# Prompt attention in one stage over pairs of heads, scores formed twice, and the gates as projection chunks

## The chip, the core and the metric

The kernel runs on one core of a Trainium2 chip. Its engines run side by side, each its own instruction queue: PE (TensorE, matmuls and transposes), ACT (ScalarE), DVE (VectorE), POOL (GpSimd) and SP (SyncE, which here issues DMAs). Matmuls read SBUF and write PSUM, eight banks of 512 f32 columns; ACT and DVE read PSUM, POOL does not. The metric is the device time of one execution in microseconds.

## What is computed

One step of a two-layer encoder, for a prompt of 1,024 tokens and for 8 streams of 16 tokens with caches of 512. A layer projects the tokens, runs three kinds of attention with 8 heads of 64 each (A: forgetting attention, causal; B: a sliding window with sinks; C: latent attention, chunk-causal), gates each, mixes them and normalises:

```python
  h = x @ W_in  (one combined projection; columns split among all head groups and gates)
  A: forgetting attention (FoX), per-frame causal, logit[t,s] += F[t]-F[s], F = cumsum(log sigmoid(w_f.x+b_f))
  B: sliding-window GQA (window 128 = two whole chunks back + own chunk) with learned per-head sinks, rotary
  C: multi-head latent attention (RMS-normed KV latent, decoupled rotary key), block-causal chunk mask
  branch_n = W_n( mixer_n * silu(gate_n) ),  m = sum_n sigmoid(g_n) * branch_n,  y = m @ W_o
  x <- LayerNorm(alpha * x + y),  alpha = (2*DEPTH)^(1/4)
```

## The kernel before

`build` runs, for each layer, nine stages with a barrier of all engines behind each: `projections`, `forget_sums`, `latent_keys`, `prompt_attention` for A, B and C, `stream_attention`, `up_projection`, `output_projection`. Between stages data go through scratch tensors in HBM. P is 128; NT is 9 token tiles (8 of the prompt, PT, and one of the streams); KT is 8 tiles of the model width.

`projections` makes x @ W_in in 9 chunks of up to 512 columns. Products there are fp32r: weights and inputs are each split into a high and a low half (wh, wl, xh, xl), and a token tile is 8 x 3 matmuls of 512 columns (L351 to L353) with the tokens as the stationary operand. xh and xl are kept through the attention stages, because the 3,072 gate columns are left over for them.

`latent_keys` transposes the latents of each token tile and multiplies them, in f32, with the weights of C's queries, keys and values.

`prompt_attention` works on one head after the other, two in a loop turn. `prep` (L995) transposes its queries and keys to have their 64 to 96 features on partitions. `order`, a list made in Python and the same for PE, ACT and DVE, sets the sequence. For each tile `a` of 128 queries: `score` (L1009, mask L1012) makes up to 1,024 columns of scores in PSUM (ss) with queries on partitions, DVE takes the row maximum (L1133), ACT the exponential and its sum (L1091), `turn` (L1027) transposes the probabilities tile by tile, ACT and DVE copy them out, and `pv` (L1045) multiplies them with the values, 64 columns at a time. DVE divides and gates (L1172). Between these, `fill` (L1056 to L1058) makes one token tile of 256 gate columns, 24 fp32r matmuls, nine times in a loop turn; POOL splits the gate weights (L968, L970).

`up_projection` transposes the three gated outputs of each token tile on PE (L1800), splits them and multiplies with W_n (L1820 to L1822).

## Time and profile before

| | us |
|---|---|
| median of the runs shown | 3794.53 |
| lowest and highest of three | 3792.19, 3799.66 |
| the profiled execution | 3789.74 |
| its span, first instruction to last | 3788.1 |

A profile row gives an engine's busy time, a count, and in the groups the mean length of one. A PE record's length holds its way through the array, some 0.16 us, so a matmul's price is the distance from one start to the next. An f32 matmul leaves two records, an fp32r or bf16 one leaves one. `128*64` behind the names is the stationary operand, rows by columns; PEld is its load. PEclk is the granted share of the clock: 1.0 stands for 2.4 GHz, 0.5 for 1.2.

### The profile page before, as it was taken

The numbers are of one execution on the slowest core, as the hardware profiler recorded it, in microseconds if no ns is written. First come the engines' busy times: TensorE is split into PE (matmuls) and PEld (weight loads), VectorE is DVE, ScalarE is ACT, GpSimd is POOL, SyncE is SP. The second block draws the span as 40 slices with busy tenths as digits, with TensorE's granted clock in tenths as the row PEclk, the third lists the DMA queues.
The fourth block names the chain that finished last, engine by engine and source line by source line (L and its number), as shares of the span: only waits on it lengthen the run. The fifth ranks groups of instructions, "written<-read, shape, count | busy, mean of one in ns | idle before, by whom it ended". The sixth has DMA issues, their size and how long they took to land. (4 is left out here: it accounts for less than half of the span.)

```text
span 3788.1 us, 54850 instructions
## 1 busy us (share of the span) xinstructions
PE 3390.3 (89%) x20866; PEld 2834.0 (75%) x20866; DVE 1411.7 (37%) x3261; ACT 885.1 (23%) x1982; POOL 125.5 (3%) x64
## 2 busy tenths in 40 slices
PE   0999978998998997989969999789989999978988
PEld 0888865887997885667758888568879878855877
DVE  5114233333343332354631233334333333323556
ACT  1221212332222332220221112123322233322110
POOL 0000000100100000000000000000000001000000
PEclk9999988999999998989979999889999989988999
DMA  5322225221433225753442222342233243186533
GB/s 194 106 89 94 77 89 160 62 64 39 108 76 98 59 72 142 244 220 126 144 153 92 88 91 67 120 123 64 64 74 91 60 98 87 37 231 212 218 129 107
DMA packets 485460, 423.06 MB, mean 112 GB/s; under 512 B 300452, under 2 KB 394532, under 8 KB 482916
## 3 DMA queue, kind: packets, MB, share of 16 engines
q1 hardware_dynamic: 451444, 381.06, 33.7%
q10 hardware_dynamic: 33840, 39.66, 3.2%
q8 instruction: 110, 1.80, 0.2%
...
## 5 line engine op out<-in xcount | busy, mean ns | idle before, releaser
L351 PE MATMUL proj_acc<-proj_wh,keep_xh 128*128 128x512 f32 (+1 forms) x1296 | 502.1, 387 | 12.5 <-DVE proj_wl L326 12.5
L352 PE MATMUL proj_acc<-proj_wl,keep_xh 128*128 128x512 f32 (+1 forms) x1296 | 500.8, 386 | 0.0
L353 PE MATMUL proj_acc<-proj_wh,keep_xl 128*128 128x512 f32 (+1 forms) x1296 | 500.7, 386 | 0.0
L351 PEld LDWEIGHTS proj_acc<-proj_wh,keep_xh 128*128 128x128 f32 x1296 | 244.5, 189 | 58.4 <-DVE proj_wl L326 13.3
L352 PEld LDWEIGHTS proj_acc<-proj_wl,keep_xh 128*128 128x128 f32 x1296 | 244.6, 189 | 45.7
L353 PEld LDWEIGHTS proj_acc<-proj_wh,keep_xl 128*128 128x128 f32 x1296 | 244.4, 189 | 45.7
L1820 PE MATMUL up_acc<-up_wh,up_bh 128*128 128x512 f32 x432 | 173.1, 401 | 12.8 <-DVE up_wl L1864 12.8
L326 DVE TENSOR_TENSOR proj_wl<-proj_raw,proj_wh 128x512 fp32r<-128x512 f32 (+1 forms) x144 | 96.1, 676 | 210.6 <-ACT proj_wh L321 210.6
L1056 PE MATMUL att_c_gacc<-att_c_gwh,keep_xh 128*128 (+1 forms) x576 | 170.7, 296 | 2.9 <-DVE att_c_gwl L1185 2.9
L1056 PE MATMUL att_b_gacc<-att_b_gwh,keep_xh 128*128 (+1 forms) x576 | 170.7, 296 | 2.3 <-DVE att_b_gwl L1185 2.3
L1056 PE MATMUL att_a_gacc<-att_a_gwh,keep_xh 128*128 (+1 forms) x576 | 169.9, 295 | 1.9 <-DVE att_a_gwl L1185 1.9
L1821 PE MATMUL up_acc<-up_wl,up_bh 128*128 128x512 f32 x432 | 170.4, 394 | 0.0
L1822 PE MATMUL up_acc<-up_wh,up_bl 128*128 128x512 f32 x432 | 170.2, 394 | 0.0
L1057 PE MATMUL att_c_gacc<-att_c_gwl,keep_xh 128*128 (+1 forms) x576 | 164.7, 286 | 0.0
L1057 PE MATMUL att_b_gacc<-att_b_gwl,keep_xh 128*128 (+1 forms) x576 | 164.6, 286 | 0.0
L1058 PE MATMUL att_c_gacc<-att_c_gwh,keep_xl 128*128 (+1 forms) x576 | 164.6, 286 | 0.0
L1058 PE MATMUL att_b_gacc<-att_b_gwh,keep_xl 128*128 (+1 forms) x576 | 164.5, 286 | 0.0
L1057 PE MATMUL att_a_gacc<-att_a_gwl,keep_xh 128*128 (+1 forms) x576 | 163.9, 285 | 0.0
L1058 PE MATMUL att_a_gacc<-att_a_gwh,keep_xl 128*128 (+1 forms) x576 | 163.6, 284 | 0.0
L1091 ACT ACTIVATE att_a_p<-att_a_ss,att_a_stat 128x128 f32<-128x128 f32 (+7 forms) x128 | 95.1, 743 | 255.5 <-DVE att_a_stat L1133 255.4
L1091 ACT ACTIVATE att_c_p<-att_c_ss,att_c_stat 128x128 f32<-128x128 f32 (+7 forms) x128 | 95.1, 743 | 252.9 <-DVE att_c_stat L1133 252.9
L1009 PE MATMUL att_a_ss<-att_a_kt,att_a_qt 66*128 66x512 f32 (+3 forms) x384 | 148.3, 495 | 1.7 <-DVE att_a_kt L1128 1.7
...
## 6 DMA issues: line engine op xcount, KB each, us to landing
...
```

The costliest lines, as they stand in the source:

```text
L326: nc.vector.tensor_tensor(wl[:, u, kt, 0:w], raw[:, kt // 2, kt % 2, 0:w], wh[:, u, kt, 0:w].bitcast(F32), ALU.subtract).then_inc(w_ready[ ...
L351: nc.tensor.matmul(bank, hi, wh[:, u, kt, 0:w], start=kt == 0, stop=False)
L352: nc.tensor.matmul(bank, hi, wl[:, u, kt, 0:w], start=False, stop=False)
L353: mm = nc.tensor.matmul(bank, lo, wh[:, u, kt, 0:w], start=False, stop=kt == KT - 1)
L1009: nc.tensor.matmul(ss[:, s, c:c + cw], lhs, kt[:, u, first + c:first + c + cw], start=True, stop=not last)
L1056: nc.tensor.matmul(gacc[:, 0:GW], hi, wh, start=kt_ == 0, stop=False)
L1057: nc.tensor.matmul(gacc[:, 0:GW], hi, wl, start=False, stop=False)
L1058: mm = nc.tensor.matmul(gacc[:, 0:GW], lo, wh, start=False, stop=kt_ == KT - 1)
L1091: nc.scalar.activation(p[:, s, 0:w], ss[:, s, 0:w], ACT.Exp, bias=stat[:, s, 0:1], accum_out=stat[:, s, 1:2]).then_inc(exp_ready, 1)
L1820: nc.tensor.matmul(acc[:, a, :], bh[:, u, k, :], wh[:, k, cols], start=k == 4 * n, stop=False)
L1821: nc.tensor.matmul(acc[:, a, :], bh[:, u, k, :], wl[:, k, cols], start=False, stop=False)
L1822: mm = nc.tensor.matmul(acc[:, a, :], bl[:, u, k, :], wh[:, k, cols], start=False, stop=k == 4 * n + 3)
```

## The change

The gates are projected in `projections`, as six more chunks of 512 columns (15 in all), with ACT's Tanh on the way out; the fills and POOL's splitting are gone. Queries, keys and the three silu gates of the prompt are projected turned over (`turned_tile`: weights stationary, tokens moving), so that features come out on partitions, and are stored so; output p_a_k is turned back on the host. The order of the chunks changes.

`latent_keys` makes its products in fp32r with three matmuls each and writes queries and keys with features on partitions, in two halves of 512 tokens. w_uq comes with the rotary columns a second time, swapped.

`prompt_attention` is one stage for A, B and C over 12 units, each a pair of heads. The two heads of a pair lie on partitions 0 to 63 and 64 to 127 and go to two tiles of the PE array (`tile_position`). Scores are formed twice. `highest` forms them with queries on partitions, for one chunk of up to 512 keys, into hs (two banks, one per head); DVE reduces both at once. Transposed and split in two halves, the maxima become rows (mrow). `score` forms the scores again with keys on partitions, adds the negated maxima as a product with ones on 32-row tiles, and ACT takes the exponential into one of four buffers p. `value` multiplies the values (stationary, 64 columns, one tile of columns a head) with them. POOL adds the probabilities up over key tiles, a matmul with ones (`add_up`) adds over partitions, and DVE takes the reciprocal of 512 columns and multiplies. A's forget sums enter `highest` as 32-row products (frow), C's rotary part as 96-row ones. `attention_order` sets the sequence: a unit's maxima are formed among the scores of the unit before.

`up_projection` loads prompt rows that are already turned; only the stream tile is transposed.

```diff
-    ("aq", [(O_AQ, 512)]), ("ak", [(O_AK, 512)]), ("av", [(O_AV, 512)]),
-    ("silu_a", [(O_AG, 512)]), ("bq", [(O_BQ, 512)]), ("silu_b", [(O_BG, 512)]),
-    ("silu_c", [(O_CG, 512)]),
...
+    ("av", [(O_AV, 512)]), ("bq", [(O_BQ, 512)]),
+    *[(f"gate{g}", [(O_GATE + 512 * g, 512)]) for g in range(6)],
+    ("silu_a", [(O_AG, 512)]), ("silu_b", [(O_BG, 512)]), ("silu_c", [(O_CG, 512)]),
+    ("aq", [(O_AQ, 512)]), ("ak", [(O_AK, 512)]),
     ("cq_bk", [(O_CQ, QR), (O_BK, 128)]),
     ("bv_ckv", [(O_BV, 128), (O_CKV, KR + RP), (O_AF, H)]),
 ]
...
...
+            def turned_tile(k, u, t):
+                if t >= 4:
+                    pe.wait_ge(out_ready[u], NT * k + t - 3)
+                bank = acc[:, 4 * u + t % 4, :]
+                block, half = slice(t // 2 * P, t // 2 * P + P), slice(t % 2 * 512, t % 2 * 512 + 512)
+                for kt in range(KT):
+                    nc.tensor.matmul(bank, wh[:, u, kt, block], xh[:, kt, half], start=kt == 0, stop=False)
+                    nc.tensor.matmul(bank, wh[:, u, kt, block], xl[:, kt, half], start=False, stop=False)
+                    mm = nc.tensor.matmul(bank, wl[:, u, kt, block], xh[:, kt, half], start=False, stop=kt == KT - 1)
+                mm.then_inc(acc_ready, 1)
...
+                chunk(c // 2, c % 2, WIDTH[c], c in TURNED)
...
+                    elif kind.startswith("gate"):
+                        nc.scalar.activation(out[:, j, :], bank, ACT.Tanh, scale=0.5).then_inc(out_ready[u], 1)
...
+            def three(bank, left, right, k, last):
+                (lh, ll), (rh, rl) = left, right
+                nc.tensor.matmul(bank, lh, rh, start=k == 0, stop=False)
+                nc.tensor.matmul(bank, lh, rl, start=False, stop=False)
+                return nc.tensor.matmul(bank, ll, rh, start=False, stop=k == last)
...
-                        for j, t in enumerate(tiles(a)):
-                            mm = nc.tensor.matmul(oo[:, 0:HD], pt[:, s, j * P:(j + 1) * P], v[:, u, t, :],
-                                                  start=j == 0, stop=j == len(tiles(a)) - 1)
-                        mm.then_inc(pv_made, 1)
-                    elif what == "fill":
-                        if n == 0:
-                            pe.wait_ge(gw_lo, i + 1)
-                        pe.wait_ge(g_taken, 1 + NT * i + n)
-                        first = KT * (i & 1)
-                        for kt_ in range(KT):
-                            hi, lo = (m[:, kt_, n * P:(n + 1) * P] for m in (xh, xl))
-                            wh, wl = (m[:, ds(first + kt_, 1), :].rearrange("p k n -> p (k n)") for m in (gwh, gwl))
-                            nc.tensor.matmul(gacc[:, 0:GW], hi, wh, start=kt_ == 0, stop=False)
-                            nc.tensor.matmul(gacc[:, 0:GW], hi, wl, start=False, stop=False)
-                            mm = nc.tensor.matmul(gacc[:, 0:GW], lo, wh, start=False, stop=kt_ == KT - 1)
-                        mm.then_inc(g_made, 1)
...
+def score_steps(kind):
+    if kind == "b":
+        return [(i // 2, [(j, a, 1, 256 * (a % 2) + P * (j == a)) for a in (2 * i, 2 * i + 1) for j in window(kind, a)])
+                for i in range(4)]
+    return [(g, [(j, max(j, 4 * g), 4 * g + 4 - max(j, 4 * g), 0)]) for g in range(2) for j in range(4 * g + 4)]
...
+        highest(0, c)
+    before = None
+    turns = [("turn", kind, i, half) for kind, count in (("q", H // 2), ("k", KVB)) for i in range(count) for half in range(2)]
+    for n in range(len(UNITS)):
+        m = len(steps[n])
+        for s in range(m):
+            order.append(("score", n, s))
+            if n + 1 < len(UNITS):
+                many = len(chunks[n + 1])
+                for c in range(s * many // m, (s + 1) * many // m):
+                    highest(n + 1, c)
+            if before is not None:
+                order.append(("value", *before))
+            if late and late[0][0] <= s + 12 * n:
+                order.append(("total", *late.pop(0)[1:]))
+            if before is not None and before[1] == last_step(UNITS[before[0]][0], steps[before[0]][before[1]][0]):
+                late.append((s + 12 * n + 1, before[0], steps[before[0]][before[1]][0]))
+            before = (n, s)
+            if s == (1 if m == 12 else 0):
+                order.append(("shift", n, 1))
+            if n in (1, 2) and turns:
...
+                    col = 256 * (a % 2) + 256 - w if kind == "b" else 0
+                    banks = [hs[:, u, col:col + w] for u in range(2)]
+                    for u in range(2):
+                        nc.tensor.matmul(banks[u], query_tiles(n, u, a), keys_of(n, u, at, w), start=first, stop=False,
+                                         skip_group_check=True, tile_position=(u * HD, 0))
+                    masked = at + w == (a + 1) * P
+                    if kind == "a":
+                        for u in range(2):
+                            g = 32 * (2 * (pair % 2) + u)
+                            mm = nc.tensor.matmul(banks[u], ones_r[g:g + 32, :], frow[g:g + 32, pair // 2, at:at + w],
+                                                  start=False, stop=not masked, skip_group_check=True, tile_position=(g, 0))
+                    elif kind == "c":
+                        for u in range(2):
+                            mm = nc.tensor.matmul(banks[u], qs[0:3 * RP, n % RQ, u, rows(a)], ks[:, at:at + w],
+                                                  start=False, stop=not masked, skip_group_check=True)
+                    if masked:
+                        wide = min(w, C[f"mask_{kind}"].shape[1])
+                        for u in range(2):
+                            mm = nc.tensor.matmul(banks[u][:, w - wide:w], C["ident16"][:],
+                                                  C[f"mask_{kind}"][:, C[f"mask_{kind}"].shape[1] - wide:],
...
+                    pe.wait_ge(mrow_ready, 2 * n + half + 1)
+                if i >= 2:
+                    pe.wait_ge(exp_ready, i - 1)
+                banks = [st[:, i % 2, u, :] for u in range(2)]
+                for j, a, many, at in blocks:
+                    for u in range(2):
+                        nc.tensor.matmul(banks[u][:, at:at + many * P], keys_of(n, u, j * P, P), query_tiles(n, u, a, many),
+                                         start=(j, a) == blocks[0][:2], stop=False, skip_group_check=True, tile_position=(u * HD, 0))
+                for j, a, many, at in blocks:
+                    for u in range(2):
+                        mm = nc.tensor.matmul(banks[u][:, at:at + many * P], ones_r[32 * u:32 * u + 32, :],
+                                              mrow[32 * u:32 * u + 32, (2 * n + half) % 4, (a - 4 * half) * P:(a - 4 * half + many) * P],
+                                              start=False, stop=False, skip_group_check=True, tile_position=(32 * u, 0))
+                    if kind == "c":
+                        for u in range(2):
+                            mm = nc.tensor.matmul(banks[u][:, at:at + many * P], ks[:, rows(j)],
+                                                  qs[0:3 * RP, n % RQ, u, a * P:(a + many) * P],
+                                                  start=False, stop=False, skip_group_check=True)
+                    if kind == "b":
+                        cols = slice(P, 2 * P) if j == a else slice(0, P)
+                    else:
+                        cols = slice(0, P)
+                    if kind == "b" or j == a:
+                        for u in range(2):
+                            mm = nc.tensor.matmul(banks[u][:, at:at + P], C[f"mask_{kind}"][:, cols], C["ident16"][:],
+                                                  start=False, stop=True, skip_group_check=True)
+                mm.then_inc(st_made, 1)
...
+                    pe.wait_ge(vs_loaded[n % 2], 32 * (n // 2 + 1))
+                fresh = s == 0 or steps[n][s - 1][0] != half
+                if fresh and 2 * n + half:
+                    pe.wait_ge(oo_taken, 2 * n + half)
+                for j, a, many, at in blocks:
+                    at_q = (a - 4 * half) * P
+                    for u in range(2):
+                        cols = slice(0, HD) if kind == "b" else heads[u]
+                        mm = nc.tensor.matmul(oo[heads[u], at_q:at_q + many * P], v[:, n % 2, j, cols],
+                                              p[:, i % RP_, u, at:at + many * P], start=fresh and (j, a) == blocks[0][:2],
+                                              stop=j == window(kind, a)[-1], skip_group_check=True, tile_position=(0, u * HD))
...
+                    mm = nc.tensor.matmul(misc[heads[u], :], C["ones"][:, 0:HD], total[:, half, u, :], start=True,
+                                          stop=kind != "b", skip_group_check=True, tile_position=(0, u * HD))
+                if kind == "b":
...
+                if kind == "a":
+                    for u in range(2):
+                        ins = nc.scalar.activation(p[:, i % RP_, u, 0:w], st[:, i % 2, u, 0:w], ACT.Exp,
+                                                   bias=fneg[:, blocks[0][0], 2 * pair + u:2 * pair + u + 1])
+                else:
+                    ins = nc.scalar.activation(p[:, i % RP_, :, lo:w], st[:, i % 2, :, lo:w], ACT.Exp)
...
                 if kind != "b":
+                    (a, at, w), = chunks[n][c]
+                    nc.vector.tensor_reduce(mneg[:, n % 2, at // 512, a, :], hs[:, :, 0:w], AXX, ALU.max, negate=True)\
+                        .then_inc(hs_taken, 1)
...
+            def add_up(n, half):
+                dve.wait_ge(misc_made, use_of["total", n, half] + 1)
+                if 2 * n + half:
+                    dve.wait_ge(br_ready, 2 * n + half)
+                nc.vector.reciprocal(inv[:], misc[:]).then_inc(total_taken, 1)
+                dve.wait_ge(total_taken, totals.index(("total", n, half)) + 1)
+                if n >= 2:
+                    dve.wait_ge(br_stored[n % 2], 16 * (n // 2))
+                nc.vector.tensor_tensor(br[:, n % 2, 512 * half:512 * half + 512], gated[:, half, :], inv[:], ALU.mult)\
+                    .then_inc(br_ready, 1)
...
+                    nc.gpsimd.tensor_tensor(sum_[:, :, cols], first[:, :, cols], mine[:, :, 0:many * P], ALU.add)\
+                        .then_inc(added, 2)
+                else:
+                    pool.wait_ge(added, i)
...
+                if t < PT:
+                    act.wait_ge(br_loaded[t % 2], 48 * (t // 2 + 1))
+                    if t >= 2:
+                        act.wait_ge(up_made, 6 * (t - 1))
+                    nc.scalar.activation(bh[:, t % 2], br[:, t % 2], ACT.Copy).then_inc(bh_made, 1)
...
-                forget_sums(nc, C, T, S, l)
-                latent_keys(nc, C, T, S, l)
-                for kind in "abc":
-                    prompt_attention(nc, C, T, S, l, kind)
...
+            forget_sums(nc, C, T, S, l)
+            latent_keys(nc, C, T, S, l)
+            prompt_attention(nc, C, T, S, l)
```

PE in the attention of A, before: in the middle of a loop turn, from the scores of one query tile over a gate fill to the next.

```order
L1009 MATMUL att_a_ss<-att_a_kt,att_a_qt 128x128
L1012 MATMUL att_a_ss<-keep_mask_a,keep_ident 128x128
L1051 REGISTER_ALU
L1056 MATMUL att_a_gacc<-att_a_gwh,keep_xh 128x256
L1057 MATMUL att_a_gacc<-att_a_gwl,keep_xh 128x256
L1058 MATMUL att_a_gacc<-att_a_gwh,keep_xl 128x256
L1056 MATMUL att_a_gacc<-att_a_gwh,keep_xh 128x256
L1057 MATMUL att_a_gacc<-att_a_gwl,keep_xh 128x256
L1058 MATMUL att_a_gacc<-att_a_gwh,keep_xl 128x256
```

Behind the eight triples of a fill stand the values of the query tile before (x7), the transposes of the probabilities (x8) and the next scores. PE in the same place now, two score steps of a unit of A:

```order
L1156 MATMUL att_st<-att_qt,att_kt 128x256 x2
L1160 MATMUL att_st<-att_mrow,att_ones_r 128x256 x2
L1174 MATMUL att_st<-keep_ident,keep_mask_a 128x128 x2
L1125 MATMUL att_hs<-att_kt,att_qt 128x384 x2
L1131 MATMUL att_hs<-att_frow,att_ones_r 128x384 x2
L1140 MATMUL att_hs<-keep_mask_a,keep_ident 128x128 x2
L1192 MATMUL att_oo<-att_p,att_v 64x384 x2
L1156 MATMUL att_st<-att_qt,att_kt 128x128 x2
L1160 MATMUL att_st<-att_mrow,att_ones_r 128x128 x2
L1174 MATMUL att_st<-keep_ident,keep_mask_a 128x128 x2
```

No fill and no transpose of probabilities is left. Each x2 is the pair of heads; L1156 and L1125 are on tiles of 64 rows, L1160 and L1131 of 32 rows, L1174 and L1140 on the full array, L1192 on tiles of 64 columns. B's score step on PE now, where the rows and the masks alternate:

```order
L1156 MATMUL att_st<-att_qtb,att_ktb 128x128 x8
L1160 MATMUL att_st<-att_mrow,att_ones_r 128x128 x2
L1174 MATMUL att_st<-keep_ident,keep_mask_b 128x128 x2
L1160 MATMUL att_st<-att_mrow,att_ones_r 128x128 x2
L1174 MATMUL att_st<-keep_ident,keep_mask_b 128x128 x2
```

The last two rows come four times in all, once per block of 128 queries and 128 keys. B formed its scores in one matmul of up to 256 columns per query tile before.

## Rows read from the trace of the kernel before

**Rows 1.** The page: its head, and PE's and DVE's busy time, share and count.

```profile
span 3788.1 us, 54850 instructions
...
PE 3390.3 (89%) x20866; PEld 2834.0 (75%) x20866; DVE 1411.7 (37%) x3261; ACT 885.1 (23%) x1982; POOL 125.5 (3%) x64
```

**Rows 2.** Busy time by stretch: projections, latent stage, attention, streaming attention, up-projection.

```profile
core 0: us, PE busy (x) PEld busy (x) DVE busy (x) ACT busy (x) POOL busy (x), PEclk, DMA share, GB/s
72.60:536.10 463.50, 447.22 (x2016) 376.83 (x2016) 129.65 (x280) 95.99 (x198) 0.00 (x0) 0.99 0.30 95
...
560.20:633.20 73.00, 69.87 (x215) 38.25 (x215) 26.39 (x88) 13.51 (x25) 0.00 (x0) 0.94 0.48 170
...
644.50:1465.40 820.90, 778.85 (x5896) 692.53 (x5896) 309.23 (x840) 248.30 (x608) 58.07 (x21) 0.97 0.29 72
...
1474.10:1612.20 138.10, 120.82 (x1030) 80.39 (x1030) 41.80 (x125) 29.86 (x73) 1.50 (x2) 0.90 0.86 250
...
1620.70:1793.10 172.40, 164.49 (x756) 135.53 (x756) 90.88 (x127) 26.96 (x39) 0.00 (x0) 0.95 0.48 179
```

**Rows 3.** The same view: start of head group A's stage, and its rest.

```profile
633.20:657.10 23.90, 10.47 (x40) 7.46 (x41) 7.81 (x20) 6.68 (x11) 0.17 (x2) 0.57 0.89 188
657.10:937.80 280.70, 274.67 (x2074) 239.96 (x2072) 108.11 (x276) 89.04 (x204) 19.26 (x6) 1.00 0.21 53
```

**Rows 4.** The same view: a stretch of projections.

```profile
190.00:285.00 95.00, 95.00 (x421) 78.67 (x420) 14.66 (x22) 20.35 (x35) 0.00 (x0) 1.00 0.26 86
```

**Rows 5.** Timeline of PE, two gate fills; start, length, engine, line, operands, count.

```profile
717.51 0.28 PE L1056 MATMUL att_a_gacc<-att_a_gwh,keep_xh 128*128 x1
717.63 0.28 PE L1057 MATMUL att_a_gacc<-att_a_gwl,keep_xh 128*128 x1
```

**Rows 6.** Timeline of PE in the latent stage, f32 of 512 columns.

```profile
586.67 1.88 PE L703 MATMUL lat_ak<-lat_wk,lat_kt 128*128 128x512 f32 x4
588.38 1.88 PE L703 MATMUL lat_av<-lat_wv,lat_kt 128*128 128x512 f32 x4
```

**Rows 7.** Timeline of PE in streaming attention: full array, 32 rows, full array.

```profile
1583.70 1.45 PE L1430 MATMUL str_ssc<-str_ktc,str_qac 128*128 128x512 f32 x3
1585.08 1.12 PE L1431 MATMUL str_ssc<-str_pct,str_qpt 32*128 32x512 f32 x2
1586.13 0.62 PE L1430 MATMUL str_ssc<-str_ktoc,str_qac 128*128 128x16 f32 x4
```

**Rows 8.** Timeline of PE: pairs of 64-row tiles side by side.

```profile
1492.95 1.16 PE L1384 MATMUL str_ssc<-str_qtc,str_wkt 64*128 64x128 f32 x16
1493.95 1.06 PE L1384 MATMUL str_tr<-str_qtc,str_wkt 64*128 64x128 f32 x16
```

**Rows 9.** Timeline of PE: four tiles of 32 columns side by side.

```profile
1588.68 1.06 PE L1404 MATMUL str_ssa<-str_ka,str_qxa 128*32 128x512 f32 x8
1589.56 0.23 PE L1404 MATMUL str_ssa<-str_ktoa,str_qxa 128*32 128x16 f32 x8
```

**Rows 10.** Timeline of PE and DVE at a reduce, with DVE's reciprocal and 512-wide copy.

```profile
712.85 0.22 PE L1012 MATMUL att_a_ss<-keep_mask_a,keep_ident 128*128 128x128 bf16 x1
...
713.11 1.22 DVE L1133 TENSOR_REDUCE att_a_stat<-att_a_ss 128x1 f32<-128x1024 f32 x1 [1.28 <-PE att_a_ss L1012]
...
716.07 0.15 DVE L1165 RECIPROCAL att_a_stat<-att_a_stat 128x1 f32<-128x1 f32 x1
...
721.17 0.69 DVE L1128 COPY att_a_pt<-att_a_tr 128x512 f32<-128x512 f32 x1 [0.59 <-PE att_a_tr L1027]
```

**Rows 11.** Groups by line and form: exp of 1,024 elements, POOL's subtraction.

```profile
L970 POOL TENSOR_TENSOR att_a_gwl<-att_a_graw,att_a_gwh 128x2048 f32 x4 | 18.1, 4513 | 0.7 <-POOL att_a_gwh L968 0.7
...
L1091 ACT ACTIVATE att_a_p<-att_a_ss,att_a_stat 128x1024 f32<-128x1024 f32 x16 | 17.9, 1120 | 39.9 <-DVE att_a_stat L1133 39.9
```

**Rows 12.** Timeline of PE: a bf16 mask and four transposes.

```profile
704.40 0.22 PE L1012 MATMUL att_a_ss<-keep_mask_a,keep_ident 128*128 128x128 bf16 x1
704.46 0.60 PE L995 MATMUL att_a_tr<-keep_ident,att_a_q 128*66 128x128 f32 x4
```

1175 lines of the change are left out of this document (672 added, 503 removed).

## The prediction

> **What bounds the kernel now.** I read the page's shares first, then the busy time by stretch, then single rows of the timeline for the price of one operation. TensorE (PE) is busy 89% of the span, no other engine over 37% [rows 1]. Cut into stages (first layer; the second repeats it within 2 us a stage), the projections keep PE busy 447 of 463.5 us and the three attention stages 779 of 821 us, gaps between them included [rows 2]. So the time is the sum of what PE issues, and the change is priced by adding up PE's work, stage by stage, and then asking where the new order makes PE wait.
>
> **Prices of one operation, from start to start.** A full-array fp32r matmul of 512 columns: 421 in 95 us, 0.226 us [rows 4]. One of 256 columns, a gate fill: 0.12 [rows 5]. An f32 matmul leaves two records, each of 0.43 us for 512 columns: a row of four starts at 586.67, the next at 588.38, 1.71 us for four [rows 6]. A transpose 0.11 (four in 0.60 us, the last one's 0.27 among it), a bf16 mask of 128 columns 0.06 [rows 12]. What is new are matmuls on parts of the array. Two tiles of 64 rows side by side: 16 records of 128 columns in 1.00 us [rows 8], where full-array ones take 16 times 0.11; the pair costs what one costs. Four tiles of 32 columns: eight records of 512 columns in 0.88 us [rows 9], two rounds of 0.43. So pairs do run together, and I take a pair at the price of one.
>
> **The price of changing tile shape.** Three f32 records of 512 columns start at 1583.70 and stream until 1583.70 + 3 x 0.429 = 1584.99; the next matmul, on 32 rows, starts at 1585.08, 0.09 later. Its two records of 0.427 would be over at 1585.93 if they streamed at once; the next full-array matmul starts at 1586.13 [rows 7]. That is 0.20 more: 0.09 again before a full shape may start and 0.11 for a weight load that nothing covers, since it too waits for the old shape to empty. 
>
> **Projections: six gate chunks more.** Each is 9 token tiles x 24 matmuls of 512 columns, 1,296 x 0.2257 = **+292.5 us a layer**, all on the path, since PE is 100% busy in such a stretch [rows 4]. Loads (2 MB per 49 us), the Tanh and the store of each tile lie under it, as those of the old chunks do. The turned tiles have as many matmuls as before: nothing.
>
> **Attention: 821 us becomes what?** Removed are 2,592 fills of 0.12 (310 us), which almost equal the gate chunks: gates alone give 18 us. The rest, some 510 us, is replaced. Per pair of heads in A and C, keys cover 36 blocks of 128x128, nine times 512 columns. Maxima, scores and values are f32 pairs: 3 x 9 x 0.858 = 23.2 us. fp32r rows (forget sums, negated maxima), on 32-row pairs: 2 x 9 x 0.226 = 4.1 in A; in C 2.0, plus four unpaired 96-row runs, 8.1. Masks 32 x 0.06 = 1.9, totals 1.7, eight transposes 0.9. A: 31.8; C: 37.8. B has 15 blocks: 3 x 15 x 0.22 = 9.9, rows 1.7, masks 3.5, totals and sinks 3.4, transposes 0.9: 19.4. Four pairs of each and 48 transposes: 127 + 151 + 78 + 5 = **361 us**, where the old kernel spent 510. So far a gain.
> Then the shapes. In the order of the new program one step goes 64 rows, 32 rows, full (mask), 64 rows, 32 rows, full, 64 columns. Counted over the stage there are 842 changes of shape a layer (A 312, C 291, B 228, the rest 11), B many because its score loop alternates a 32-row pair and a full mask per block. Each costs 0.09 plus the exposed load: 0.20 into a 128-column 32-bit load, 0.14 into 64 columns; into a bf16 mask I have no row: between 0.09 and 0.20, I take 0.12, the load being short [rows 12]. By kind: **148 us**; bounds 842 x 0.09 = 76 and 842 x 0.20 = 168.
> Then waits. The maxima go through one pair of banks (hs), so PE may not start a chunk before DVE has reduced the last. A reduce of 1,024 elements takes 1.22 us [rows 10]; in steady state value and next score (1.5 to 2.5 us with shape changes) cover it. They don't in the first unit, 12 chunks in a row: 11.5 us of reduces and 12 x 0.35 of hand-over, 16 us (the 0.35 is an estimate: the reduce at 713.11 starts 0.2 after the stream of the mask at 712.85 ends, and something less for the way back). Nor in the last B unit, which holds three chunks of C in each of four steps: 2 x 4 x 1.3 = 10. The stage starts at the lower clock, as the old one did (0.57 granted over its first 24 us, then 1.00) [rows 3], and its start-up is slower work: 12. Forget rows and first loads: 4. Sum **42 us**, bounds 20 and 80. ACT's exps are 11 to 14 us per pair (1.12 us per 1,024 elements) and POOL's additions 7,424 elements at 2.2 ns, 16 us [rows 11], against some 46 us of PE per pair: both hidden, with four p buffers between. If that cover went, PE would wait for added.
> Attention: 361 + 148 + 42 = **551**, against 821: **-270 us a layer**.
>
> **Latent stage.** 249 fp32r matmuls of 512 columns, 9 of 256 and 51 transposes: 56 + 1 + 6 = 63 us against 73 [rows 2], but it now loads half of the rows and 2.6 MB of weights and splits these before the first product: 12 to 18 us in which PE has only transposes. **+5**, bounds -5 and +15.
>
> **Up projection.** 96 of 108 transposes go, 96 x 0.11 = **-10** of 172 us, PE-bound there [rows 2]. Loads of 512-byte rows have 18 us a tile: hidden.
>
> **Sum.** 292.5 - 270 + 5 - 10 = +17.5 a layer, +35 for two. The profiled execution is 3789.7 us (span 3788.1 [rows 1]); the median is 4.8 above it. On the median: 3794.5 + 35 = **3830 us**.
>
> **Rivals.**
> 1. Forecast: every shape change is paid. With the bounds of waits and loads 3780 to 3920. Chance 0.45.
> 2. Changes of shape cost only the empty 0.09 or less, because PE pulls the load ahead when it belongs to other rows: 842 x 0.09 = 76, so -72 a layer, 3690; were they free, 3530. Against it: [rows 7] show the load exposed both ways. Chance 0.22 (0.05 for free).
> 3. Slower by a wait: DVE holds PE through hs. The new reciprocal is 512 wide, and the trace has it only at one element, 0.153 us; the nearest copy of 512 takes 0.69 [rows 10], which I used. There are 24 a layer, and all reduces stand behind them. It decides once reciprocal, product and reduce together exceed the 4 to 5 us that two steps cover, a reciprocal of over some 2.5 us; each us more then costs 24 us a layer. At 4 us: +36 a layer, 3900. 
> 4. Slower by the clock: PE empties 842 times and streams only two thirds of the stage; should a third of it run at the lower of the two levels, the 361 us grow by 120 a layer: 4070. Against it: the streaming-attention stage, full of such changes, has a mean granted clock of 0.90 of full, start-up included [rows 2]. Chance 0.08.
> 5. It doesn't do what it says: pairs of 512 columns don't overlap ([rows 8] are of 128). Maxima and scores alone add 8 x 15.4 + 4 x 6.6 = 150 a layer, 4130. Chance 0.07.
>
> **How the numbers follow.** Likeliest is 1. For 8 in 10 the range takes in rival 2 at its full 3690 (without the free case) and rival 3, and leaves out 4, 5 and free changes (0.20): 3690 to 3940. A measurement here tells about 0.2%, 8 us. Faster: rival 2 (0.22) and a fifth of case 1 (0.09), 0.31. Same: 0.07, from case 1. Slower: the other 0.29 of case 1 and cases 3 to 5 (0.33), 0.62.
>
> **What would show it.** Proj stage 756 us a layer. Between a 64-row record and the next 32-row one, 0.2 us beyond the stream. Attention stage near 551 with granted clock 1.00 after 35 us; PE waiting for DVE's reduces only in the first unit and around C's first chunks. If attention is near 480, the load is hidden; if the 512-wide reciprocal is over 2.5 us and PE waits for hs beside it, rival 3. I would be wrong at the root if PE no longer sets the end: then POOL (added) or ACT would end PE's waits.

## The result: 7.4% slower, outside the range

The changed kernel took 4081.74 us (median of four runs, 4060.77 to 4088.16) against 3795.16 us: a ratio of 1.0744 (95% interval 1.0703 to 1.0786). The forecast was 3830, the range 3690 to 3940. The direction was right, the size was not: +287 us where +35 stood.

The profiled execution took 4060.77 us, the lowest of the four; its mean granted clock is 0.909, that of the other three 0.905 or 0.906, so what is read below as lost to the clock is rather too little. The head of its page, in the form of [rows 1], and its line of the granted clock in 40 slices:

```profile
span 4059.1 us, 43586 instructions
...
PE 3573.2 (88%) x17838; PEld 2474.5 (61%) x17838; DVE 1378.4 (34%) x2063; ACT 804.9 (20%) x1410; POOL 334.7 (8%) x238
...
PEclk9999999986989878989989999999868997879899
```

Busy time by stretch in layer 1, with the columns of [rows 2]: projections, forget sums with the latent stage, attention, streaming attention, up-projection.

```profile
72.10:828.70 756.60, 740.38 (x3312) 619.89 (x3312) 162.78 (x328) 154.52 (x300) 0.00 (x0) 1.00 0.29 94
840.70:928.80 88.10, 70.63 (x325) 58.35 (x325) 28.30 (x40) 20.82 (x33) 0.00 (x0) 0.85 0.48 168
937.70:1606.40 668.70, 590.33 (x3088) 260.58 (x3088) 255.97 (x258) 144.71 (x228) 160.17 (x108) 0.84 0.15 48
1618.70:1760.20 141.50, 125.18 (x1030) 84.92 (x1030) 41.92 (x125) 29.92 (x73) 1.50 (x2) 0.86 0.83 244
1777.40:1928.90 151.50, 151.25 (x660) 124.19 (x660) 82.61 (x106) 17.40 (x16) 0.00 (x0) 0.98 0.54 184
```

The reader is to look at the third line. The stage lasts 668.7 us where 551 were forecast, PE is idle for 78 of them, and its mean granted clock is 0.84 where [rows 2] show 0.97 for the three old stages. The trace's clock records put 220 us of the stage at the lower of the two levels (1.2 GHz instead of 2.4). PE is busy for 181 us of these, so 90 us go to the clock. That splits the stage in three, and the same split is made for each run below:

| | forecast | measured |
|---|---|---|
| work at the full clock (length - idle - lost) | 361 + 148 = 509 | 668.7 - 78.3 - 90.3 = 500 |
| PE idle | 30 | 78 |
| lost to the half clock (half of PE's busy time in it) | 12 | 90 |

What PE waits for in this stage; the columns are us in total, times, the longest:

```profile
PE att_misc L1216 <- DVE att_inv L1388: 26.0, 9, 3.6
PE att_hs L1125 <- DVE att_mneg L1347: 18.8, 21, 1.3
PE att_hs L1125 <- DVE att_frow L1415: 15.3, 1, 15.3
PE att_hs L1125 <- DVE att_qs L1403: 13.7, 4, 6.1
PE att_st L1247 <- DVE att_fsrc L1339: 8.9, 1, 8.9
PE att_misc L1241 <- DVE att_inv L1388: 3.5, 1, 3.5
```

The fifth lies ahead of the stage's first matmul, the others add up to the 78. The first is the reciprocal. It shares the one bank `misc` with the sums before it and the transposes (`shift`) behind it. Timeline of PE, then of DVE: start, length, engine, line, operation.

```profile
1055.29 1.03 PE L1224 MATMUL att_misc<-att_total,keep_ones 128*64 128x512 f32 x4
1059.87 1.09 PE L1216 MATMUL att_misc<-keep_ident,att_msrc 128*128 128x128 f32 x4 [3.55 <-DVE att_inv L1388]
```

```profile
1056.37 3.36 DVE L1388 RECIPROCAL att_inv<-att_misc 128x512 f32<-128x512 f32 x1 [1.19 <-PE att_misc L1224]
1059.76 0.69 DVE L1392 TENSOR_TENSOR att_br<-att_gated,att_inv 128x512 f32<-128x512 f32 x1
```

And the clock around it, in stretches of 4 us (PEclk is the number behind POOL's):

```profile
1053.00:1057.00 4.00, 3.32 (x20) 1.20 (x18) 1.33 (x2) 1.05 (x2) 2.20 (x2) 1.00 0.77 260
1057.00:1061.00 4.00, 1.09 (x4) 0.72 (x4) 3.42 (x2) 0.01 (x1) 0.00 (x0) 0.67 0.01 2
1061.00:1065.00 4.00, 3.36 (x14) 1.96 (x16) 0.00 (x0) 1.40 (x3) 0.00 (x0) 0.50 0.33 131
1065.00:1069.00 4.00, 4.00 (x15) 1.21 (x14) 0.96 (x1) 0.62 (x2) 1.26 (x1) 0.55 0.00 0
1069.00:1073.00 4.00, 4.00 (x28) 1.92 (x25) 1.02 (x1) 1.22 (x3) 0.72 (x1) 1.00 0.00 0
```

PE stops for 3.55 us, and for 10 us from 1058.4 on it is granted half. Of the twelve half-clock stretches within the stage, behind the one at its start, eleven begin 2 to 5 us after the start of a stop of 1.6 to 6.1 us; one (at 1239.3) has no stop before it. PE had last stopped 62 us earlier:

```profile
1225.00:1239.30 14.30, 14.30 (x133) 8.60 (x134) 7.94 (x9) 3.97 (x7) 2.53 (x2) 1.00 0.10 38
1239.30:1242.70 3.40, 3.40 (x24) 2.15 (x24) 2.54 (x4) 0.82 (x3) 1.44 (x2) 0.50 0.02 5
```

Layer 2 has the same fall at the same place, 302 us into the stage, among the units of B. It comes up again under e5.

### The profile page after: what moved, and what is told of

Same layout as the page of the kernel before. It is cut to its first block and busy times, and to the rows that moved or that the text cites. A ratio compares the mean times of both kernels' runs of the same rounds, so it can differ in the third digit from the quotient of the medians.

```text
span 4059.1 us, 43586 instructions
## 1 busy us (share of the span) xinstructions
PE 3573.2 (88%) x17838; PEld 2474.5 (61%) x17838; DVE 1378.4 (34%) x2063; ACT 804.9 (20%) x1410; POOL 334.7 (8%) x238
## 5 line engine op out<-in xcount | busy, mean ns | idle before, releaser
L1347 DVE TENSOR_REDUCE att_mneg<-att_hs 128x2 f32<-128x1024 f32 (+1 forms) x192 | 183.8, 958 | 537.4 <-PE att_hs L1140 373.3
L1125 PE MATMUL att_hs<-att_kt,att_qt 64*128 64x512 f32 (+3 forms) x768 | 218.4, 652 | 96.0 <-DVE att_mneg L1347 37.6
L368 PE MATMUL proj_acc<-keep_xh,proj_wh 128*128 128x512 f32 x640 | 249.0, 389 | 0.0
L369 PE MATMUL proj_acc<-keep_xl,proj_wh 128*128 128x512 f32 x640 | 249.0, 389 | 0.0
L370 PE MATMUL proj_acc<-keep_xh,proj_wl 128*128 128x512 f32 x640 | 249.0, 389 | 0.0
L1466 POOL TENSOR_TENSOR att_total<-att_total,att_p 128x1024 f32<-128x1024 f32 (+3 forms) x128 | 206.2, 1611 | 373.5 <-ACT att_p L1283 202.5
L1192 PE MATMUL att_oo<-att_p,att_v 128*64 128x128 f32 (+3 forms) x1248 | 226.9, 471 | 0.0
L1156 PE MATMUL att_st<-att_qt,att_kt 64*128 64x512 f32 (+3 forms) x768 | 200.1, 602 | 0.0
L1388 DVE RECIPROCAL att_inv<-att_misc 128x512 f32<-128x512 f32 x48 | 161.1, 3357 | 83.1 <-PE att_misc L1224 57.2
L326 ACT ACTIVATE proj_wh<-proj_raw 128x512 fp32r<-128x512 f32 (+1 forms) x240 | 147.1, 619 | 85.5 <-PE proj_acc L358 77.0
```

Of the source, the lines that this page charges most:

```text
L368: nc.tensor.matmul(bank, wh[:, u, kt, block], xh[:, kt, half], start=kt == 0, stop=False)
L369: nc.tensor.matmul(bank, wh[:, u, kt, block], xl[:, kt, half], start=False, stop=False)
L370: mm = nc.tensor.matmul(bank, wl[:, u, kt, block], xh[:, kt, half], start=False, stop=kt == KT - 1)
L1125: nc.tensor.matmul(banks[u], query_tiles(n, u, a), keys_of(n, u, at, w), start=first, stop=False, skip_group_check=True, tile_position=(u ...
L1156: nc.tensor.matmul(banks[u][:, at:at + many * P], keys_of(n, u, j * P, P), query_tiles(n, u, a, many), start=(j, a) == blocks[0][:2], stop ...
L1192: mm = nc.tensor.matmul(oo[heads[u], at_q:at_q + many * P], v[:, n % 2, j, cols], p[:, i % RP_, u, at:at + many * P], start=fresh and (j, ...
```

## Experiments on the waits

All of these are edits of the changed kernel. The first takes the reciprocal's length away, the second only its hold on the bank. In what was expected of the runs, theory 1 is that PE's stops bring the clock down, theory 2 that the changes of tile shape do.

```diff
-                nc.vector.reciprocal(inv[:], misc[:]).then_inc(total_taken, 1)
+                nc.vector.tensor_copy(inv[:], misc[:]).then_inc(total_taken, 1)
```

> The changed kernel with the 24 reciprocals a layer of 512 columns (3.36 us each) replaced by a copy (0.69 us); the division is left out. In its profile the attention stage of layer 1 takes 668.7 us: PE idle 78 us, of which 29.5 wait for the reciprocal to give back the bank misc, and PE busy 181 us while the granted clock is at half, which is 90 us more than at full clock. Theory 1 (the clock falls because PE stood still): the 29.5 us go and with them most of the half-clock stretches that begin just behind these waits (82 to 116 us long in sum, half of that lost): 65 to 80 us less a layer, the kernel 130 to 160 us faster than the changed one, near 3930 to 3950. Theory 2 (the clock falls because the changes of tile shape keep PE emptying, waits or not): only the waits go, 27 to 32 us a layer, near 4020, and the mean clock of the stage stays at 0.84. Theory 3 (the reciprocal's length is hidden and the wait would be taken over by something else): under 10 us a layer.

Measured: 3913.17 us (ratio to the kernel before 1.0323, interval 1.0305 to 1.0340), 169 us less than the changed kernel. The stages take 595 and 611 us, PE idle 50 in each, 39 and 58 lost to the clock. Theory 1 put the gain at 130 to 160, theory 2 at 60: the clock came back with the waits. Work at full clock is 504 to 506, as it was.

```diff
                 nc.vector.tensor_copy(inv[:], misc[:]).then_inc(total_taken, 1)
                 dve.wait_ge(total_taken, totals.index(("total", n, half)) + 1)
+                ch.link(nc.vector.reciprocal(inv[:], inv[:]))
```

> The changed kernel, but DVE first copies misc to inv (0.69 us, gives the bank back) and takes the reciprocal in place in SBUF behind it. If what counts is the bank that PE waits for before the transposes of the shift, this gives nearly what the copy alone gives in the run before (within 10 us a layer). If it is DVE's time, which the reduces of hs share, the waits move to the reduces: the 29.5 us a layer come back as waits on the reduce, and the gain is under 20 us a layer. My guess: two thirds of the gain of the copy, 45 us a layer, near 3990.

Measured: 3944.25 us (1.0414, 1.0388 to 1.0441), 137 us less. The stages take 610 and 614 us, PE idle 60 and 61, 45 and 48 lost to the clock. So four fifths of what the copy alone gives come from giving the bank back 2.7 us earlier, though DVE is held 0.7 us longer each time. The guess was 90 us; the bank was the greater part of it.

Next the stop of 15.3 us at the start. Timeline of DVE there:

```profile
955.03 0.17 DVE L1412 TENSOR_SCALAR att_nsink<-att_sink 128x8 f32<-128x8 f32 x1 [17.36 <-DMA att_sink<-in_sinks]
955.24 1.29 DVE L1415 CAST att_frow<-att_st 128x512 fp32r<-128x512 f32 x2
```

DVE's queue has the negated sinks ahead of the forget rows, and the sinks (4 KB) are loaded behind 3 MB of B's rows. The edit moves `sp.dma_start(sink[:], ...)` to the front of SP's queue.

> The changed kernel with the load of the sinks moved from behind the 3 MB of head group B's rows to the front of SP's queue. In the changed kernel DVE stands 17.4 us at the sinks' load with the copy of the forget rows behind it, and PE waits 15.3 us for these. Theory 1a: that wait goes and nothing else, 13 to 15 us a layer; the clock stays at half until the first unit is over, since its chunks are each followed by a wait of 0.5 to 1.3 us for the reduce. Theory 1b: with the long wait gone the clock rises 20 us into the stage as in the old kernel, and the first unit's 53 us shrink by another 20: 33 us a layer. Rival: the first loads of q and k (6 to 8 us to landing) take over, under 8 us a layer.

Measured: 4060.59 us (1.0700, 1.0682 to 1.0718), 21 us less, with an uncertainty of some 17 from the two intervals. The wait is gone (0.9 us left) and PE's idle time falls by 15 us a layer, 30 in all. That fits theory 1a (26 to 30 us for both layers) and rules out 1b (66).

The profiles cannot say what the clock did with it. The two stages (673.2 and 672.6 us, 113 and 111 lost to the clock) are no shorter than the changed kernel's, but here an execution of 4068.58 us was profiled, above its median, and there one of 4060.77, 21 us under it. How far the same work varies is seen in the probes e9, e10, e12 and e13 below, which leave the attention stage as it is: with the changed kernel's own two, these ten stages take 667.7 to 687.3 us and lose 89 to 111 us to the clock. A difference of some 20 us between the losses in two profiles can therefore not be put down to an edit.

One thing this profile does show: a stretch of 31 us in which PE is never idle, at 0.51:

```profile
993.00:1024.00 31.00, 31.00 (x96) 10.48 (x94) 7.39 (x9) 4.59 (x9) 6.39 (x5) 0.51 0.00 1
```

```diff
-                if i >= 1:
+                if n == 0:
+                    if i >= 2:
+                        pe.wait_ge(hs_taken, i - 1)
+                elif i >= 1:
                     pe.wait_ge(hs_taken, i)
...
-                    banks = [hs[:, u, col:col + w] for u in range(2)]
+                    banks = [highest_bank(n, c)[:, u, col:col + w] for u in range(2)]
...
+    def highest_bank(n, c):
+        return st[:, 1] if n == 0 and c % 2 else hs
...
```

> The changed kernel, but the 12 chunks of maxima of the first pair alternate between hs and one half of st, which nobody uses yet; the rest is as it was. The ten waits of 0.5 to 1.3 us in the first unit (9.8 us) go. Theory 1 (waits hold the clock down): the clock rises in the course of the first unit and it takes 53 - 10 - 10 to 20 = 23 to 33 us: 20 to 30 us less a layer. Theory 2 (changes of shape hold it down): the clock stays at half as long as the first unit runs, 8 to 10 us less a layer.

Measured: 4042.45 us (1.0658, 1.0612 to 1.0704), 39 us less, with an uncertainty of some 24. That lies between the two theories' ends (40 to 60 and 16 to 20 us for both layers) and does not decide between them. PE's idle time falls by 8.4 us a layer; the stages take 652.6 and 669.2 us and lose 82 and 101 to the clock. In layer 1 the clock rises for the first time at 974 us instead of 1010.6, 36 us into the stage for 73; but in e9, with the attention stage untouched, it does so after 43.

## Experiments on the changes of shape

The price of a change first. In B's score step rows and masks alternate, with nothing between; timeline of PE:

```profile
1326.37 0.33 PE L1160 MATMUL att_st<-att_mrow,att_ones_r 32*128 32x128 f32 x2
1326.63 0.29 PE L1174 MATMUL att_st<-keep_ident,keep_mask_b 128*128 128x128 bf16 x2
1326.84 0.33 PE L1160 MATMUL att_st<-att_mrow,att_ones_r 32*128 32x128 f32 x2
1327.10 0.28 PE L1174 MATMUL att_st<-keep_ident,keep_mask_b 128*128 128x128 bf16 x2
1327.32 1.13 PE L1125 MATMUL att_hs<-att_kt,att_qt 64*128 64x512 f32 x4
1328.38 0.73 PE L1135 MATMUL att_hs<-att_ks,att_qs 96*128 96x512 f32 x2
```

From row to row 0.47 us, of which some 0.17 are streaming: 0.30 for two changes, 0.32 forecast. The last two rows show a full-width pair on half arrays: four records in 1.06 us, that is two rounds of 0.43 and 0.20 for the change. So pairs overlap at 512 columns (rival 5 is out), and neither is the load hidden nor a change free (rival 2 is out).

```diff
                 for j, a, many, at in blocks:
                     for u in range(2):
                         mm = nc.tensor.matmul(banks[u][...], ones_r[32 * u:32 * u + 32, :], mrow[...])
...
+                for j, a, many, at in blocks:
                     if kind == "b" or j == a:
                         for u in range(2):
                             mm = nc.tensor.matmul(banks[u][:, at:at + P], C[f"mask_{kind}"][:, cols], C["ident16"][:])
```

> The changed kernel, but head group B's score step forms the rows of all its blocks first and then all its masks, where rows and masks alternated: 96 changes of tile shape less a layer (842 become 746). In the changed kernel a pair of 32-row matmuls and a pair of masks take 0.47 us together, of which 0.17 is streaming: 0.15 us a change. Forecast: 14 us a layer less, near 4053. If the load of a mask were hidden (0.09 a change), 9 us a layer.

Measured: 4051.36 us (1.0683, 1.0644 to 1.0722), 30 us less, 14 a layer forecast. The trace counts 754 changes, not 746, and the work at full clock is 487 and 489 us for 500: 12 us for 88 changes.

The profile of e5 also answers what the fall at 1239.3 was. The kernels in which B's rows and masks alternate (the changed one, e1 to e4, e7, e9, e10, e12, e13) give twenty profiled stages. In seventeen the clock falls among B's units though PE has not stopped for 58 us or more; in both stages of e1 and one of e7 it does not. In e5, with the same waits and B's rows and masks grouped, PE works through B without a stop for over 100 us in both layers, and there is no such fall:

```profile
1226.00:1240.00 14.00, 14.00 (x134) 8.24 (x130) 5.00 (x10) 4.56 (x10) 4.84 (x6) 1.00 0.19 57
1240.00:1244.00 4.00, 4.00 (x46) 2.82 (x45) 3.93 (x4) 1.40 (x3) 0.61 (x1) 1.00 0.00 0
```

Nor is there one in the ten stages of the kernels below that group them as well (e6, e8, e11, e14, e15), though in these PE also stops more often among B's units. So the clock comes down without any stop too, if not every time, and the likely cause are changes of shape as dense as B's (one each 0.24 us in the rows above); with three of twenty stages free of it, two of e5 are few to show that. It is a small part: 3.4 of the 220 us at half clock in the changed kernel's layer 1.

For the next, the rows of the negated maxima and the forget sums stand on rows 0 and 64 (and 32, 96), and a selector of ones and zeros `two_r` on tiles of 64 rows picks them; PE's loop takes a score step and the chunk behind it apart:

```diff
+                elif what == "score":
+                    score_rows(*of)
+                    if todo and todo[0][0] == "highest":
+                        nxt = todo.pop(0)[1:]
+                        highest_rows(*nxt)
+                        score_full(*of)
+                        highest_full(*nxt)
+                    else:
+                        score_full(*of)
```

> The changed kernel with the same products, but the rows of the negated maxima and of the forget sums are on tiles of 64 rows like the scores, and a score step and the chunk of maxima behind it give all their 64-row matmuls first and then all that are on the full array: 393 changes of tile shape a layer for 842. All of its waits are left as they are. At 0.15 to 0.2 us a change: 67 to 90 us a layer less at full clock, some of which the waits for the reduces take back. Theory 1 (waits hold the clock down): PE is idle as long as before or longer and still loses some 90 us a layer to the half clock: 55 to 70 us a layer less, near 3955. Theory 2 (the changes of shape hold it down): the loss falls with their number to some 42 us: 110 to 120 us a layer less, near 3850.

Measured: 3870.44 us (1.0206, 1.0183 to 1.0228), 211 us less, with 394 changes of shape in the trace. And its counterpart, all shapes left and the waits seen to (e2, e3 and e4 together, and C's position rows split some steps earlier):

> The changed kernel with all 842 changes of shape, but with its four waits taken care of: misc copied before the reciprocal, the sinks loaded first, the first unit's chunks alternating between hs and st, and the split of head group C's position rows put some steps earlier. The waits of PE in the attention stage fall from 78 to about 30 us a layer. Theory 1: with them goes most of the half-clock time (181 us busy at half clock become 60 to 90): 90 to 110 us a layer less, near 3880. Theory 2: only the waits, 48 us a layer, near 3985, the mean clock near 0.84.

Measured: 3867.97 us (1.0193, 1.0176 to 1.0210), 214 us less. Then both:

> Both edits of the two runs before together. If they add up: the stage takes 500 us of work at full clock less 67 to 90 for the shapes, 30 to 45 of waits, 30 to 45 lost to the half clock: 490 to 520 us for 668.7, the kernel near 3750, one per cent faster than the old one. If fewer changes of shape bare the reduces (a chunk of maxima, a step of scores and a step of values then take 3.5 us less cover for 1.22 us of reduce and 4.7 us of reciprocal work), PE waits for hs and the gain over fewer waits alone is under 40 us a layer, near 3810.

Measured: 3748.62 us (0.9874, 0.9855 to 0.9892): 46 us faster than the kernel before. The attention stage of layer 1 in these four kernels, the changed one's line being shown above; fewer shapes, fewer waits, both:

```profile
938.69:1511.48 572.79, 483.29 (x3088) 249.83 (x3088) 251.54 (x258) 144.01 (x228) 160.59 (x108) 0.88 0.17 55
```

```profile
938.87:1519.02 580.15, 553.05 (x3088) 248.27 (x3088) 272.05 (x281) 144.70 (x228) 161.28 (x108) 0.91 0.17 56
```

```profile
938.82:1451.83 513.01, 465.80 (x3088) 242.55 (x3088) 275.23 (x281) 143.33 (x228) 163.66 (x108) 0.94 0.20 62
```

| layer 1 | stage | idle | lost to the clock | work at full clock |
|---|---|---|---|---|
| changed kernel | 668.7 | 78 | 90 | 500 |
| fewer shapes | 572.8 | 90 | 48 | 435 |
| fewer waits | 580.2 | 27 | 49 | 504 |
| both | 513.0 | 47 | 28 | 438 |

The last column behaves as it should: 448 changes fewer save 65 us, 0.145 each, and the waits do not touch it. The column before it settles theory 1 against theory 2 by refuting both in their plain form. With the waits left alone (even 12 us more of them) fewer shapes halve the loss; with the shapes left alone fewer waits halve it too. Fewer shapes gave 106 us a layer (theory 1: 55 to 70, theory 2: 110 to 120), fewer waits 107 (theory 1: 90 to 110, theory 2: 48). Both kinds of emptiness count. The differences of 41 to 42 us in the loss are well beyond the 22 us by which untouched stages differ, and layer 2 repeats them (50, 56 and 30 us lost for 90). The gains a layer are halves of the medians' differences; the two stages profiled differ by less (96 and 89 us in layer 1), since the changed kernel's profiled execution lies 21 us under its median.

## Probes of the clock in a place of its own

The 40 turned projection tiles a layer are dense: in the changed kernel they run from 493.7 to 732.8 us, 239 us at a granted 1.00. There each cause can be put in by itself.

```diff
                     mm = nc.tensor.matmul(bank, wl[:, u, kt, block], xh[:, kt, half], ...)
+                    if kt < KT - 1:
+                        nc.tensor.matmul(bank[:, 0:16], C["ident16"][0:32, :], C["ident16"][0:32, 64:80],
+                                         start=False, stop=False, tile_position=(0, 0))
```

> A probe in a place without any wait: in the 40 projection tiles a layer that leave the silu gates and q and k turned (8 times three matmuls of 512 columns each, PE 100% busy at full clock in the changed kernel), a matmul of 16 columns on a tile of 32 rows, which adds zero to the same bank, stands behind each of the first seven threes: 280 of them, 560 changes of tile shape a layer, one each 0.5 us, as dense as in the attention stage. Price: each pair of changes takes 0.4 us at 0.09 and a bare load of 0.11 (0.3 if one load hides), 112 us a layer, if the clock stays at full. If changes of shape alone pull the clock down, the stretch shows a granted clock well under 1.00 and costs up to twice as much, over 200 us a layer. Theory 1 says it stays at 1.00, theory 2 that it falls; after the runs with fewer waits and with fewer shapes, each of which halved the loss, I give the fall 0.4.

Measured: 4269.0 us (1.1251, 1.1228 to 1.1273). The stretch takes 331 us, 92 more (112 forecast): 0.164 a change, one change each 0.59 us, and it kept the full clock throughout, in both layers:

```profile
562.36 0.39 PE L370 MATMUL proj_acc<-keep_xh,proj_wl 128*128 128x512 f32 x1
562.69 0.18 PE L372 MATMUL proj_acc<-keep_ident 32*128 32x16 bf16 x1
562.79 0.50 PE L368 MATMUL proj_acc<-keep_xh,proj_wh 128*128 128x512 f32 x1
...
490.00:824.00 334.00, 334.00 (x1351) 204.34 (x1350) 43.61 (x67) 47.80 (x84) 0.00 (x0) 1.00 0.21 66
```

The small matmul starts 0.33 after the one before it (0.23 of streaming, 0.10 of emptying) and the next 0.10 later, which then streams for 0.34 to its successor, a bare load of 0.11 in it.

```diff
-                if t >= 4:
-                    pe.wait_ge(out_ready[u], NT * k + t - 3)
+                if t >= 1:
+                    pe.wait_ge(out_ready[u], NT * k + t)
```

> The counterpart: the same 40 tiles a layer, no change of shape, but PE may start a tile only when the one before has been written out of its bank (it could be three ahead before). So each tile of 5.4 us is followed by a wait of some 1.5 to 3 us. Waits: 35 times 2 us, 50 to 100 us a layer. If waits alone pull the clock down, the stretch is granted under 1.00 by half of its time and the tiles in it take up to 10.9 us instead of 5.4; if it takes both, the clock stays at 1.00. I expect it to fall here and there, the mean of the stretch at 0.8.

Measured: 4187.28 us (1.1035, 1.1013 to 1.1058). The waits came out shorter than I had guessed, and the clock did not fall. The waits in the stretch, and the stretch:

```profile
PE proj_acc L368 <- DVE proj_out L482: 29.6, 21, 1.4
PE proj_acc L368 <- ACT proj_out L433: 9.6, 14, 0.7
...
490.00:783.00 293.00, 253.76 (x1075) 198.69 (x1074) 44.10 (x67) 48.28 (x85) 0.00 (x0) 1.00 0.24 76
```

So 35 stops of 0.7 to 1.4 us, each 6 to 7 us, cost themselves and the refilling (50 us in all) and nothing through the clock. The reciprocal's stops are longer:

```diff
+                if t in (1, 5):
+                    pe.wait_ge(out_stored[(t - 1) % 3], 16 * (3 * (2 * k + u) + (t - 1) // 3 + 1))
```

> The changed kernel; in the same 40 turned projection tiles PE waits twice a chunk until the tile before has been stored to HBM, ten waits a layer of some 3.5 us, as long as those for the reciprocal, with more than 20 us of dense matmuls between; no change of shape. Theory 1 in its strict form (one long stop is enough): the clock falls to half behind each, as it did 2 to 5 us behind eleven stops of 1.6 to 6.1 us in the attention stage: 35 us of waits and 30 to 60 us of lost clock a layer. If it takes a stop and thin streaming around it: the clock stays at 1.00, 35 us a layer. I give the latter 0.6.

Measured: 4162.32 us (1.0965, 1.0817 to 1.1113; executions of 4139 and 4185 us, the first of them profiled), the stretch 285 us. Ten stops of 2.7 to 3.4 us; behind six of them the clock falls to half, for 3.4 us each, once 6.8: 24 us in all. Around the third:

```profile
560.00:563.00 3.00, 0.23 (x1) 0.23 (x2) 1.29 (x2) 0.50 (x1) 0.00 (x0) 1.00 0.23 87
563.00:567.00 4.00, 4.00 (x13) 3.14 (x13) 0.00 (x0) 0.00 (x0) 0.00 (x0) 0.65 0.00 0
567.00:571.00 4.00, 4.00 (x18) 3.25 (x17) 0.18 (x1) 0.81 (x2) 0.00 (x0) 0.92 0.00 0
```

Layer 2 has the half clock behind six of its ten stops too, and they are not the same six: twelve of twenty. I had given 0.6 to the clock staying up. One long stop is often enough, in the densest company. With the changes of shape of e9 around the same stops:

> Both in one place: the ten waits of the run before and the 560 changes of shape of e9 in the 40 turned projection tiles. If the clock falls where PE streams thinly and also stops, as in the attention stage, the stretch shows 0.80 to 0.90 here though it kept 1.00 with the changes alone; more than 92 + 35 us a layer, by 20 to 60. If it keeps 1.00 here too, neither the changes nor the stops explain the attention stage's clock, and something of its matmuls must (pairs on half arrays, f32 in two passes).

Measured: 4365.18 us (1.1500, 1.1409 to 1.1591). All ten stops are now followed by the half clock, 48 us in all, twice as much as without the changes; in layer 2 again all ten, 44 us. The stretch in e13, then in e12:

```profile
494.70:878.10 383.40, 351.97 (x1338) 210.74 (x1337) 43.44 (x66) 47.79 (x85) 0.00 (x0) 0.94 0.18 56
494.40:779.50 285.10, 253.65 (x1058) 205.44 (x1057) 43.40 (x66) 47.81 (x84) 0.00 (x0) 0.96 0.24 75
```

It takes 383 us, 144 more than undisturbed: 92 for the changes, 31 for the waits, 21 for the clock. The forecast was 20 to 60 beyond the first two, and a granted clock of 0.80 to 0.90, where 0.94 was measured. That is the attention stage's main pattern: the stop brings the clock down, and thin streaming made that certain here and let it last longer. In the attention stage a stop of 3.6 us is followed by 3 to 17 us at half.

## What remained of the reciprocal

> The kernel of e8 (fewer shapes and fewer waits) with the copy alone and no reciprocal behind it; the division is left out. It measures what DVE's 3.35 us twenty-four times a layer still cost there. In e8 PE waits 24.6 us a layer for the reduces, of which some nine stand behind a reciprocal, 2 us each at C's units: 10 to 14 us a layer with the clock behind it, 3748 becomes 3720 to 3730. If the reciprocal were hidden by now: no difference.

Measured: 3673.58 us (0.9678, 0.9662 to 0.9695), 75 us less than e8, where 20 to 28 were expected. PE's waits for the reduces fall from 24.6 to 10.1 us in layer 1, the loss to the clock from 28 to 13. Of the 37 us a layer, 19 are waits and 15 are clock (9 in layer 2); I had again priced the waits at little more than their own length. Two kernels then looked for these 75 us. The first gives the division to ACT:

```diff
+                nc.scalar.activation(inv[:, k % 2], misc[:], ACT.Ln).then_inc(total_taken, 1)
+                act.wait_ge(total_taken, k + 1)
+                nc.scalar.activation(inv[:, k % 2], inv[:, k % 2], ACT.Exp, scale=-1.0).then_inc(inv_ready, 1)
```

> The kernel of e8, but the division leaves DVE: ACT forms Ln of misc and then Exp with scale -1 (0.6 us each at 512 columns), DVE only multiplies, after the next reduce. With the copy in place of the reciprocal (e11) the kernel took 3673.6 us, 75 less than e8, so that is what can be had, and DVE gives back another 0.69 each. But the trace of the changed kernel shows a table load of 1.28 us at each change between Exp and Ln (three at lines 622, 624 and 1280): two for each of the 24 totals would make ACT's part 3.8 us, and the exponentials of the next step, with two buffers of scores, come that much later. If the loads occur, PE waits for exp_ready, 1 to 3 us each: near 3740, between 3700 and 3800. If they do not: near 3665.

Measured: 3698.25 us (0.9740, 0.9711 to 0.9768). The table loads are there, two for each total:

```profile
L1349 ACT ACT_TABLE_LOAD x24 | 30.8, 1283 | 0.4
L1351 ACT ACT_TABLE_LOAD x24 | 30.8, 1283 | 0.4
```

but they are all but hidden: PE waits 7.9 us in the stage for ACT to give `misc` back, where in e8 it waits 7.0 for DVE, and 0.2 for late exponentials. The forecast with these loads, near 3740, was too high. The second leaves the work on DVE and cuts it up: the copy of `misc` at once, then `reciprocal` on columns 0 to 255 behind the next reduce, on 256 to 511 and the product behind the one after.

> The kernel of e8 with the same work on DVE in another order: the copy of misc at once, and the reciprocal as two of 256 columns (1.7 us each), one behind each of the next two reduces, the product behind the second. If what still costs is how long DVE is held in one go (4.0 us behind the copy, with a reduce waiting), most of the 75 us between e8 and e11 come back: 40 to 60, near 3700. If it is DVE's time in all, nothing: 3748.

Measured: 3699.07 us (0.9757, 0.9735 to 0.9778), as forecast, and level with e14. The reciprocals take DVE no less than in e8, where 24 of 3.35 us make 80.5; the group in the attention stage now:

```profile
L1443 DVE RECIPROCAL att_inv<-att_inv 128x256 f32<-128x256 f32 x48 | 82.4, 1734 | 0.1
```

Yet 50 of the 75 us are back: what cost was the length in one piece, with a reduce queued behind it.

Either is 2.5% faster than the kernel before.

## The prediction, point by point

- **Projections.** +292.5 us a layer forecast, 756.6 - 463.5 = 293.1 measured.
- **Latent stage, up-projection.** The stages themselves did better than forecast: 67.6 us for 72.9 where +5 stood, 151.4 for 172.4 where -10 stood (the old stage was idle for 8 us inside, this one for 0.2). But two first loads that I called hidden or left out came late: PE waits 16.8 us for the latents where it waited 8.6, and 17.3 us at the start of the up-projection for the split weights where it waited 8.6 for a load. With these, all that is not attention comes to +284 a layer from start to start; 287.5 were forecast.
- **Attention: the whole miss.** -148 a layer from start to start instead of -270. The work at full clock came out, 500 us for 509, in part by luck: at the 0.145 a change measured on the 448 that e6 removes, 842 changes are 122 us and not 148, so the streaming was some 378 and not 361, and the two misses cancel in part. The two terms behind it failed, by 48 and 78 us a layer. Without them the profiled execution would lie 19 us above the old one's 3789.7, where +35 stood: the direction did not hang on them.
- **The term of the waits,** 30 of the 42 (bounds of the whole 20 and 80), 78 measured. Its part for the reduces was rather too high, 26 for 18.8. The step "Forget rows and first loads: 4" missed the sinks' load in DVE's queue, 15.3 us; the split of C's position rows, another 13.7, had no term at all. The reciprocal was priced at a copy, 0.69; it takes 3.36. Rival 3 had its length nearly right (4 us) and the price of its waits (+36 a layer beside 29.5 waited), but its mechanism only in part: it said that reduces would be late in hs, while PE stood at the bank `misc`, 3.5 us at a time (e2). I had listed who writes hs and not who shares misc. The estimate worked out from the Trainium skill, "VectorE: DVE Perf Modes", First, the fixed hardware budget (a repeat count of 8 for Reciprocal), 4.3 us, was nearer than my row; the traces give 3.36 us for 512 columns and 1.73 for 256, so the time does go by the element, if somewhat faster.
- **The clock,** 12 us in the forecast, 90 measured. The term took the clock for a matter of the stage's start and put nothing for falls behind later stops. Rival 4 named it, with 120, at a chance of 0.08, and argued against it with streaming attention's 0.90. Its extent was right: a third of the stage, 220 of 669 us, ran at the lower level. That row was a sign for it: a stage of thin streaming that did not hold its clock. Its cause, changes of shape alone, was too narrow: eleven of the twelve falls stand behind stops, and shapes aggravate these (e12, e13). It was not wrong altogether: one change each 0.59 us did nothing to the clock (e9), among B's, one each 0.24 us, it came down without a stop in 17 of 20 stages.
- **The range.** It took the rivals one at a time. Rivals 3 and 4 happened together, because the one's waits are in the main the other's trigger, and their sum, with what else was late, lies 142 us beyond its end.
- **Signs named beforehand.** 756 us for the projections and 0.2 us behind a 64-row record came out; "granted clock 1.00 after 35 us" and "waiting for reduces only in the first unit and around C's first chunks" did not.

Open remain why the fall without a stop is missing in three of twenty stages and whether the density of changes is its whole cause; what the matmuls' own form (pairs on half arrays, f32) adds, which no probe took apart; how much of e6's effect on the clock comes from the number of changes, since it also moves the rows to 64-row tiles and changes the order within a step; and whether e3 and e4 changed anything in the clock.
